# A decoder trunk on one core: sums over partitions by 32x32 transposes on VectorE and four products instead of eight

## The reference, cut to what matters

```python
cond = jax.nn.silu(c)
for l in range(DEPTH):
    mod = cond @ w_mod[l] + b_mod[l]
    sh1, sc1, g1, sh2, sc2, g2 = jnp.split(mod[:, None, :], 6, axis=-1)
    u = x * (1.0 + sc1) + sh1
    ...   # mixed: projection, attention, convolution, group norm
    x = _layer_norm(DEEPNORM_ALPHA * x + (1.0 + g1) * (mixed @ w_out[l]), ln1_g[l], ln1_b[l])
    u = x * (1.0 + sc2) + sh2
    ff = jnp.square(jax.nn.relu(u @ w_ff1[l])) @ w_ff2[l]
    x = _layer_norm(DEEPNORM_ALPHA * x + (1.0 + g2) * ff, ln2_g[l], ln2_b[l])
```

## Time and profile before

| what | value |
|---|---|
| three runs | 2361.34, 2363.52, 2365.28 us, median 2363.52 |
| the profiled execution | 2359.68 us, its span 2358.0 us |
| busy share of the span | PE 96%, PEld 80%, DVE 73%, ACT 47%, POOL 10% |
| chain that ended last | PE 87%, DVE 6%, DMA 3%, issue 2%, ACT 1% |
| mean granted clock of TensorE | 0.99 |
| HBM traffic | 264 GB/s over the span |

### The profile page before, as it was taken

How to read it: one execution, slowest core, us unless ns; L and a number is a source line. 1 busy time by engine, 2 the same in 40 slices (tenths; PEclk the granted TensorE clock), 3 DMA queues, 4 the chain that set the end, 5 groups by cost and what they waited for, 6 DMA issues and landing times.

```text
span 2358.0 us, 30332 instructions
## 1 busy us (share of the span) xinstructions
PE 2275.1 (96%) x10480; PEld 1884.4 (80%) x10480; DVE 1727.1 (73%) x1929; ACT 1101.9 (47%) x1392; POOL 227.3 (10%) x400
## 2 busy tenths in 40 slices
PE   3899999999999999999999999999999999999997
PEld 2777887878888888888878888877888888888886
DVE  6889888877777777668878878777666555555566
ACT  1345543366445445435454554435553543543542
POOL 3311111110001001001010001101000000000000
PEclk9899999999999999999999999999999999999999
DMA  9987888967888888888966888886677776666574
GB/s 379 409 318 274 311 320 313 341 216 255 286 297 287 285 285 300 288 276 289 323 228 196 271 265 288 285 273 224 194 238 239 226 231 212 215 205 195 170 232 133
DMA packets 174734, 623.15 MB, mean 264 GB/s; under 512 B 19728, under 2 KB 20496, under 8 KB 174096
## 3 DMA queue, kind: packets, MB, share of 16 engines
q1 hardware_dynamic: 114128, 407.50, 50.6%
q0 software_dynamic: 55296, 201.35, 25.6%
q10 hardware_dynamic: 5184, 12.59, 1.7%
HBM read 619.27 MB, written 2.10 MB: 264 GB/s over the span
## 4 chain that ended last, share of the span: by engine, by line
PE 87%; DVE 6%; DMA 3%; issue 2%; ACT 1%; ACTq 0%; POOL 0%; DVEq 0%; SPq 0%; POOLq 0%
PE bank L1323 27%; PE bank L1325 26%; PE bank L1324 26%; DMA Z<-w_mod_dram 2%; DVE mod_acc L808 2%; PE bank L1428 2%; DVE w_lo L793 1%; PE bank L1337 1%; PE bank L1403 1%; PE bank L1339 1%; PE bank L1338 1%; ACT w_hi L480 1%; PE bank L1412 1%; DMA raw<-w_out_dram 0%; PE bank L1572 0%
## 5 line engine op out<-in xcount | busy, mean ns | idle before, releaser
L480 ACT ACTIVATE w_hi<-raw 128x1024 fp32r<-128x1024 f32 x764 | 807.6, 1059 | 1135.7 <-PE bank L1325 1015.2
L793 DVE TENSOR_TENSOR w_lo<-raw,w_hi 128x1024 fp32r<-128x1024 f32 x764 | 932.9, 1224 | 550.7 <-ACT w_hi L480 548.9
L1323 PE MATMUL bank<-w_hi,u_hi 128*128 128x512 f32 x1744 | 698.0, 400 | 0.3 <-DVE u_lo L851 0.3
L1325 PE MATMUL bank<-w_lo,u_hi 128*128 128x512 f32 x1744 | 684.1, 392 | 0.0
L1324 PE MATMUL bank<-w_hi,u_lo 128*128 128x512 f32 x1744 | 684.0, 392 | 0.0
L1323 PE MATMUL bank<-w_hi,m_hi 128*128 128x512 f32 x1200 | 470.9, 392 | 4.5 <-DVE m_lo L851 2.6
L1324 PE MATMUL bank<-w_hi,m_lo 128*128 128x512 f32 x1200 | 468.4, 390 | 0.0
L1325 PE MATMUL bank<-w_lo,m_hi 128*128 128x512 f32 x1200 | 468.3, 390 | 0.0
L1325 PEld LDWEIGHTS bank<-w_lo,u_hi 128*128 128x128 f32 x1744 | 330.5, 189 | 70.7
L1323 PEld LDWEIGHTS bank<-w_hi,u_hi 128*128 128x128 f32 x1744 | 330.9, 190 | 68.8 <-issue 1.4
L1324 PEld LDWEIGHTS bank<-w_hi,u_lo 128*128 128x128 f32 x1744 | 331.0, 190 | 68.0 <-issue 1.4
(11 more groups left out here) (144 smaller groups left out, 1138.3 us busy)
## 6 DMA issues: line engine op xcount, KB each, us to landing
raw<-w_ff_dram SPq DMA_DIRECT2D x512, 512.0 KB, 4.2
mod_raw<-w_mod_dram POOLq DMA_DIRECT2D x320, 512.0 KB, 5.6
raw<-w_in_dram SPq DMA_DIRECT2D x192, 512.0 KB, 5.3
Z<-w_mod_dram POOLq DMA_DIRECT2D x64, 512.0 KB, 11.0
raw<-w_out_dram SPq DMA_DIRECT2D x64, 512.0 KB, 6.1
gate<-b_rows_dram ACTq DMA_DIRECT2D x4, 1024.0 KB, 5.0
Z<-ln_g_dram ACTq DMA_DIRECT2D x16, 256.0 KB, 6.5
Z<-ln_b_dram ACTq DMA_DIRECT2D x16, 256.0 KB, 7.3
```

The source lines that it names most:

```text
L480: nc.scalar.activation(weights(w_hi, u_hi, unit, j), raw[:, j % RAW, :], ACT.Copy).then_inc(hi_ready, 1)
L793: nc.vector.tensor_tensor(weights(w_lo, u_lo, unit, j), raw[:, j % RAW, :], weights(w_hi, u_hi, unit, j).bitcast(F32), ALU.subtract).then_ ...
L1323: nc.tensor.matmul(o, hi[:, k, tok], wh, start=(k == 0), stop=False)
L1325: ins = nc.tensor.matmul(o, hi[:, k, tok], wl, start=False, stop=(k == KC - 1))
```

## The change

The shifts' and scales' slabs are summed over partitions in two steps. On VectorE, right behind the sixteenth step of such a slab, `quarter_sums` takes each half (512 columns) of `mod_acc`, transposes its 32x32 blocks into `turned_acc`, and adds 32 neighbouring columns of that, which leaves 16 numbers on each partition; both halves give `part`, 128x32. There each quarter of 32 partitions holds its own sum for each column. On TensorE `quarter_slab` replaces `reduce_slab`: four products with 128x128 windows of a 0/1 matrix `quad` (128x224, loaded with the other small tables) add the four quarters and put each column's sum on its partition. They stand at the same label, accumulate in one bank of eight columns, and wait for `part_ready` in place of `mod_used`. The bias is added as before. Gates and the start are as they were.

```diff
+        quad = sb("quad", [P, 7 * 32])
+        turned_acc = sb("turned_acc", [P, NCOL])
+        part = sb("part", [P, 32])
...
-            small = [(cs[:], cos), (sn[:], sin), (msk[:], mask), (mixg[:], mix_g), (cw[:], conv_w), (lnc[:], ln_cols)]
+            small = [(quad[:], quads), (cs[:], cos), (sn[:], sin), (msk[:], mask), (mixg[:], mix_g), (cw[:], conv_w), (lnc[:], ln_cols)]
...
-            act.wait_ge(small_in, 16 * 6)
+            act.wait_ge(small_in, 16 * 7)
...
+            def quarter_sums(n):
+
+                a = mod_acc[:, n % 2, :]
+                dve.wait_ge(mod_used, (n + 1 - START_SLABS) * KC + START_SHARE)
+                for i in range(2):
+                    sync(nc.vector.transpose(turned_acc[:], a[:, i * NCOL:(i + 1) * NCOL]))
+                    ins = nc.vector.tensor_reduce(part[:, 16 * i:16 * (i + 1)],
+                                                  turned_acc[:].rearrange("p (b j) -> p b j", j=32), AX_X, ALU.add)
+                    if i == 0:
+                        sync(ins)
+                    else:
+                        ins.then_inc(part_ready, 1)
+
             def mods(p):
 
                 for q, at in enumerate(MOD_AT):
                     if at == p:
                         mod_next(q)
+                        n = START_SLABS + q // KC
+                        if q % KC == KC - 1 and n not in GATE_SLABS:
+                            quarter_sums(n)
...
-                        dve.wait_ge(small_in, 16 * 6)
+                        dve.wait_ge(small_in, 16 * 7)
...
-            def reduce_slab(par, job, steps):
-
-                b = begin_job(job)
-
-                pe.wait_ge(mod_used, steps)
-                for c in range(SC):
-                    ins = nc.tensor.matmul(b[:, c:c + 1], mod_acc[:, par, c * P:(c + 1) * P], ones[:, 0:1],
-                                           start=True, stop=True)
-                ins.then_inc(t_done, 1)
...
-                    reduce_slab(n % 2, JOB[("red", n)], (n + 1 - START_SLABS) * KC + START_SHARE)
+                    quarter_slab(JOB[("red", n)], sum(1 for m in range(START_SLABS, n + 1) if m not in GATE_SLABS))
+
+            def quarter_slab(job, count):
+
+                b = begin_job(job)
+                pe.wait_ge(part_ready, count)
+                for r in range(4):
+                    ins = nc.tensor.matmul(b[:, 0:SC], quad[:, 96 - 32 * r:224 - 32 * r], part[:].rearrange("p (q r) -> p r q", r=4)[:, r, :],
+                                           start=(r == 0), stop=(r == 3))
+                ins.then_inc(t_done, 1)
...
+    lane = np.arange(P)
+    quads = (lane[:, None] % 32 + 96 == np.arange(7 * 32)[None, :]).astype(np.float32)
```

More of the change, by code:

```diff
@@ L199, in transpose_jobs, with build @@
     return at
-def build(nc, x, cond_c, ln_cols, w_in, w_out, w_ff1, w_ff2, w_mod, b_mod, b_rows, conv_w, mix_g, ln1_g, ln1_b,
+def build(nc, x, cond_c, ln_cols, w_in, w_out, w_ff1, w_ff2, w_mod, b_mod, quads, b_rows, conv_w, mix_g, ln1_g, ln1_b,
           ln2_g, ln2_b, cos, sin, mask, ident, out):
@@ L301, in build @@
         mod_used = sem("mod_used")
+        part_ready = sem("part_ready")
         cond_exp = sem("cond_exp")
@@ L1679 @@
         "b_mod": b_mod.reshape(SLABS * SC, P).T,
+        "quads": quads,
         "b_rows": b_mod.reshape(DEPTH, 2, 3, D)[:, :, 2].reshape(DEPTH * 2, D),
```

## The result

The changed kernel takes 2381.03 us (median of four runs), the kernel before 2363.61: 17.4 us more, a ratio of 1.0083 with the interval 1.0071 to 1.0095. A later comparison gave 2382.4 against 2362.2, 1.0092 (1.0075 to 1.0110). The direction and the place were as forecast; the size was not: 9.5 us were forecast, and 17 to 20 came. The time lies above the 2368 to 2378 that the forecast gave as its own range.

What follows compares the result with a forecast made beforehand. TensorE, 87% of the chain, was taken as the bound. Saved products -10.2, stalls +17.75, squares +1.65 and load +0.3 gave +9.5 us, median 2363.5 to 2373.0; own range 2368 to 2378, 8 in 10 range 2363 to 2387.

Steps and rivals of the forecast that it cites:

- the products: On TensorE, four products replace eight in each of 12 slabs, saving 0.85 us a slab, 10.2 us in all.
- waits at the products: TensorE idles ahead of the new products: 8.0 us over six slabs, 2.85 at slab 8, 1.6 at 18 to 20, 2.5 at 21.
- slab 9's weight split: VectorE's last weight split of the unit ends later behind the sums, so TensorE stalls 2.8 us at that tile.
- squares behind slab 6: VectorE's delayed multiplication puts back ScalarE's square, so TensorE's sums of squares after slab 6 stall a further 1.65 us.
- larger load at the start: 112 KB more are loaded at the start while the DMA engines are full, adding 0.3 us.
- The bound, the place, the sign: TensorE holds 87% of the chain; new waits on VectorE at twelve slabs outweigh the products' saving, making the kernel slower.
- Q: VectorE's path from a slab's last accumulation step to its finished partial sums: 2.85 us, between 2.35 and 4.05.
- The rivals with a short or a slow transpose: VectorE's transposes and sums: short gives 2357 us, chance 0.09; slow transposes give 2387 us, chance 0.13.
- the one on the products' price: Rival: an eight-column matmul on TensorE costs twice a one-column one, so nothing is saved: +19.7 us, 2383; chance 0.03.
- the short case: Rival: VectorE transposes and sums at line 804's rate, Q about 1.3 us, total -6.45 us, 2357; chance 0.09.
- The covers: Gap from VectorE's last step to TensorE's products, less 0.15 us handover: 1.52 at slab 6, 0 at 8, 0.35 at 21.
- TensorE stands still for Q less the cover: Each wait ahead of a slab's products was priced at Q minus that slab's cover, for example 1.33 us at slab 6.

Runs made afterwards that it cites:

- the last version: Changed kernel with each slab's partial sums and products moved to labels where VectorE has idle time, slab 20's behind the second group's squares: 2352.96 us against 2361.61, 0.9963.

## Why the prediction was right or wrong

The terms of the sum, forecast and measured (starts of matmuls in the two profiles of the changed kernel against the first one of the kernel before):

| term | forecast | first profile | second profile |
|---|---|---|---|
| the products | -10.2 | 12 x (0.89 - 1.70) = -9.7 | -9.7 |
| waits at the products | +14.95 | five of 1.41, 1.69, 2.93, 0.68, 0.53, 0.49, 2.46 = +15.8 | +15.6 |
| slab 9's weight split | +2.8 | +2.7 | +2.7 |
| squares behind slab 6 | +1.65 | +1.3 | 0 |
| larger load at the start | +0.3 | +0.3 (first group at 42.88, before 42.59) | +0.4 |
| half clock behind these waits | none | +8.0 | +11.1 |
| sum | +9.5 | +18.4 | +20.1 |

The spans of the two first profiles differ by 21.9, more than the 18.4: outside these places the changed kernel's profile has half-clock stretches at the ends of the mixers and MLPs (1.1, 2.2, 0.7 and 1.5 us) that the first one of before lacks, and somewhat shorter waits elsewhere. The medians, 17.4 and 20.2 apart, are the better measure.

- **The bound, the place, the sign: right.** TensorE's stream sets the end, and a longer wait on VectorE at the same label turned a saving into a loss. The two halves alone show it: 8.2 us faster without the sums, 9.9 slower with nothing but the sums.
- **Q: right.** 2.94 against 2.85. The price of the transpose, which had no row, was taken from the 512-column subtraction, and 0.712 us is near that. The estimate from the Trainium skill, "VectorE: DVE Perf Modes", section "The three transpose paths", was 0.711, and the trace agrees. The rivals with a short or a slow transpose fall with it, and so does the one on the products' price (0.89 for eight matmuls). Some of the prediction's sums are off without changing the forecast: its terms give Q = 2.83, the rate of line 804 gives the short case a Q of 1.6 and not 1.3 (some 2359 us, not 2357), and its list has eleven covers that a Q of 2.35 would relieve, not ten.
- **The covers: right to some tenths**, slab for slab. Slab 8 waits 2.93 longer than before, slab 21 2.46, slabs 18 to 20 0.68 to 0.49.
- **Slab 9: right.** The split that ended ahead of 479.19 comes late, as VectorE's and TensorE's timelines of the changed kernel show:

```profile
484.08 0.69 DVE L828 TENSOR_REDUCE part<-turned_acc 128x16 f32<-128x512 f32 x1
484.68 1.22 DVE L797 TENSOR_TENSOR w_lo<-raw,w_hi 128x1024 fp32r<-128x1024 f32 x1
...
483.01 0.39 PE L1359 MATMUL bank<-w_lo,m_hi 128*128 128x512 f32 x1
485.95 0.51 PE L1357 MATMUL bank<-w_hi,m_hi 128*128 128x512 f32 x1 [2.55 <-DVE w_lo L797]
```

- **The squares behind slab 6: right in the first profile**, 1.16 us of idle time released by ScalarE's square, where the earlier trace rows had 0.22 from square to product:

```profile
321.45 1.06 ACT L699 ACTIVATE Z<-Z 128x1024 f32<-128x1024 f32 x1 [5.23 <-DVE Z L1130]
...
322.56 0.60 PE L1591 MATMUL bank<-ones,Z 128*128 128x1 f32 x4 [1.16 <-ACT Z L699]
```

In the second profile this wait is gone: slab 6 has a half-clock stretch there, TensorE comes 1.6 us later, and the square is done. TensorE's waits for the squares in the first and the second profile, of which one of 1.1 us stands in the kernel before too:

```profile
PE bank L1591 <- ACT Z L699: 2.3, 2, 1.2
PE bank L1591 <- ACT Z L699: 1.1, 1, 1.1
```

- **The step that failed: "TensorE stands still for Q less the cover".** A wait was priced at its length. It also brings a stretch at half clock in five of the twelve cases in one profile and seven in the other, some 1.6 us each, and the sum lacked that term altogether; at 8.0 and 11.1 us it is about as large as the forecast itself. Keeping TensorE busy through the waits gave most of it back (2374.4), which is the direct test. The trace of before held the warning: its TensorE matmuls stand 0.43 apart behind the wait that ends at 395.77, where nothing but a 1.3 us wait and small products went ahead:

```profile
395.77 1.95 PE L1572 MATMUL bank<-ones,Z 128*128 128x1 f32 x16 [1.14 <-ACT Z L695]
...
397.96 0.63 PE L1324 MATMUL bank<-w_hi,m_lo 128*128 128x512 f32 x1
398.38 0.63 PE L1325 MATMUL bank<-w_lo,m_hi 128*128 128x512 f32 x1
```

The Trainium skill, "TensorE: Matmul & The Clock Gate", Part 1, says that a monitor sets the clock to half or full by how busy TensorE has lately been; the trace agrees (0.50 behind the wait, 1.00 where it was filled).
- **One profile as the base.** The first profile of before had no half clock at three ends of a mixer or MLP; its second profile had, and was 5.8 us longer. Differences of single profiles carry that much.
- **The range: in part luck.** The time lies within the 8 in 10 range, but its upper part, to 2387, was there for slow transposes, which didn't come. What brought the time there was the half clock, for which the prediction had neither a term nor a rival.

## What to carry to other kernels

Work taken off the busiest engine is no gain if its remainder waits for a longer chain elsewhere: read the cover at each place, the time between the producer's end and the consumer's start, and move the consumer back until it holds the new chain, as the last version did for 8.7 us. Price a new idle wait of TensorE at its length and a share of a half-clock stretch behind it, which here nearly doubled the loss. And look for what stands behind the inserted work on its own engine (here one weight split and one square): moving one slab's sums behind the split was worth 5 us.

## What the runs showed of the hardware

- Waits of 1.4 us in a stream that was otherwise full were followed by some 3 us at the lower clock in some executions and not in others, at the same place with the same wait (slabs 6 and 7). Each such stretch cost some 1.6 us. With the waits filled by idle products none of eleven slabs had one, in one profile.
- Small matmuls behind a wait of the same length drew it more often when there were sixteen with one column (nine slabs, one profile) than eight with eight columns (five and seven, two profiles).
- On VectorE a 32x32-block transpose of 128x512 f32 takes 0.712 us and a sum of 16 times 32 columns 0.686, near a two-input subtraction of that size (0.691).
